# Mixture-of-experts stage: plain float32 products on unsplit weights, in column tiles, experts ranked on chip by their row count

## The reference, cut to what matters

```python
g_sel = jnp.argmax(g_logits, axis=-1)
e_in = jnp.take_along_axis(e_logits, g_sel[:, None, None], axis=1)[:, 0]
top_v, top_i = lax.top_k(e_in, TOP_K)                       # TOP_K = 2
expert_id = g_sel[:, None] * EXPERTS_PER_GROUP + top_i      # 32 experts
combine = jnp.sum(one_hot(expert_id, N_EXPERTS) * w_top[..., None], axis=1)
hg = jnp.einsum('td,edf->tef', t, w_gate)                   # d = 1024, f = 256
hu = jnp.einsum('td,edf->tef', t, w_up)
act = jax.nn.silu(hg) * hu * combine[:, :, None]
y = jnp.einsum('tef,efd->td', act, w_down)
```

## Time and profile before

| | us |
|---|---|
| median of 3 runs (1365.02 to 1366.16) | 1366.15 |
| span of the profiled execution, first to last instruction | 1363.2 |
| TensorE busy, share of the span | 1309.7, 96% |
| expert stage, first product to last | 1028.3 to 1344.6 |
| behind the last product | 18.6 |

### The profile page before, as it was taken

The page is one execution under the profiler, slowest core; times in us unless marked ns, Lnnn a source line. Parts: engine busy times, 40 slices in busy tenths (PEclk is TensorE's granted clock), DMA queues, the critical chain, the costliest instruction groups (busy, mean ns, idle before and its releaser), DMA issues.

```text
span 1363.2 us, 23818 instructions
## 1 busy us (share of the span) xinstructions
PE 1309.7 (96%) x9405; PEld 1202.4 (88%) x9405; DVE 1032.2 (76%) x1535; ACT 872.8 (64%) x1289; POOL 78.2 (6%) x81
## 2 busy tenths in 40 slices
PE   7999999999999999999999899999998999999994
PEld 7989999998999998999999888999986777777773
DVE  6776655568555568998998886874569999999994
ACT  6565444546444546675656766654457999999994
POOL 0001000001000000000001100110000111011113
PEclk9999999999999999999999999999999999999997
DMA  8644555553655544555435534454436999999963
GB/s 276 205 152 130 191 185 185 185 186 94 202 185 187 187 140 145 178 161 158 150 102 181 193 122 155 155 186 161 157 156 254 365 360 354 351 366 365 362 261 123
DMA packets 150108, 279.78 MB, mean 205 GB/s; under 512 B 13721, under 2 KB 122238, under 8 KB 136574
## 3 DMA queue, kind: packets, MB, share of 16 engines
q1 hardware_dynamic: 141952, 269.97, 57.0%
q0 software_dynamic: 7696, 8.41, 2.0%
q10 hardware_dynamic: 366, 0.12, 0.0%
HBM read 274.26 MB, written 21.50 MB: 217 GB/s over the span
## 4 chain that ended last, share of the span: by engine, by line
PE 75%; DVE 15%; ACT 5%; issue 3%; DMA 1%; ACTq 0%; DVEq 0%; POOLq 0%; POOL 0%; SPq 0%
PE psum L852 18%; PE psum L854 18%; PE psum L853 18%; DVE weights_parts L2692 3%; PE psum L1413 3%; PE psum L1412 3%; PE psum L1411 3%; DVE weights_parts L2086 2%; PE psum L1437 2%; DVE arena L2476 2%; PE psum L1439 2%; PE psum L1438 2%; ACT weights_parts L1933 1%; ACT weights_parts L1476 1%; PE psum L1256 1%
## 5 line engine op out<-in xcount | busy, mean ns | idle before, releaser
L2086 DVE TENSOR_TENSOR weights_parts<-ring,weights_parts 128x1024 fp32r<-128x1024 f32 (+3 forms) x312 | 363.4, 1184 | 161.5 <-ACT weights_parts L1476 161.1
L1476 ACT ACTIVATE weights_parts<-ring 128x1024 fp32r<-128x1024 f32 (+3 forms) x312 | 309.0, 1010 | 175.6 <-PE psum L854 174.8
L852 PE MATMUL psum<-xnorm_parts,weights_parts 128*128 128x256 f32 x884 | 255.5, 289 | 6.0 <-DVE xnorm_parts L2235 2.0
L853 PE MATMUL psum<-xnorm_parts,weights_parts 128*128 128x256 f32 x884 | 249.0, 282 | 0.0
L854 PE MATMUL psum<-xnorm_parts,weights_parts 128*128 128x256 f32 x884 | 248.9, 282 | 0.0
L852 PE MATMUL psum<-expert_cols,weights_parts 128*128 128x256 f32 (+1 forms) x688 | 194.7, 283 | 3.3 <-DVE expert_cols L2104 2.0
L854 PE MATMUL psum<-expert_cols,weights_parts 128*128 128x256 f32 (+1 forms) x688 | 192.1, 279 | 0.0
L853 PE MATMUL psum<-expert_cols,weights_parts 128*128 128x256 f32 (+1 forms) x688 | 191.9, 279 | 0.0
L852 PE MATMUL psum<-hidden_parts,weights_parts 128*128 128x256 f32 x640 | 181.9, 284 | 2.6 <-DVE hidden_parts L2544 1.7
L853 PE MATMUL psum<-hidden_parts,weights_parts 128*128 128x256 f32 x640 | 180.5, 282 | 0.0
L854 PE MATMUL psum<-hidden_parts,weights_parts 128*128 128x256 f32 x640 | 180.5, 282 | 0.0
(11 more groups left out here) (422 smaller groups left out, 2528.3 us busy)
## 6 DMA issues: line engine op xcount, KB each, us to landing
expert_raw<-in_w_exp_down SPq DMA_DIRECT2D x35, 1024.0 KB, 7.6
ring<-in_mlp_w_up SPq DMA_DIRECT2D x32, 1024.0 KB, 5.4
ring<-in_mlp_w_down SPq DMA_DIRECT2D x32, 1024.0 KB, 4.9
ring<-in_w_in SPq DMA_DIRECT2D x30, 1024.0 KB, 5.3
ring<-in_w_exp_gate SPq DMA_DIRECT2D x23, 1024.0 KB, 5.0
ring<-in_w_exp_up SPq DMA_DIRECT2D x23, 1024.0 KB, 7.3
ring<-in_attn_w_qkv SPq DMA_DIRECT2D x12, 1024.0 KB, 8.4
expert_raw<-in_w_exp_gate SPq DMA_DIRECT2D x12, 1024.0 KB, 5.0
```

The source lines that it names most:

```text
L852: pe.matmul(out, lh, rh, start=start, stop=False, **more)
L853: pe.matmul(out, lh, rl, start=False, stop=False, **more)
L1476: ins = act.activation(high, src, ACT.Copy)
L2086: ins = dve.tensor_tensor(low, src, high.bitcast(F32), ALU.subtract)
```

## The change

The stage no longer splits the weights. Each product is a plain float32 matmul on the loaded matrix, with the expert's rows as the stationary operand and the weights as the moving one.

A block now has 64 or 32 rows. The output of a 64-row block takes half of the array's columns, so two products stand side by side: for `gate_up` gate in columns 0 to 63 and up in 64 to 127, each with 256 moving columns; for `down` the two halves of the result with 512 each. A 32-row block has four such column tiles, with 128 moving columns in `gate_up` and 256 in `down`.

Expert 0 is fixed at first place, rank 0, and loaded ahead of the routing. The other 31 are ranked on chip by row count. The expert of rank r has at most 512 / r rows, so a fixed table gives each rank its blocks: four of 64 rows for ranks 0 to 2, three for rank 3, two for ranks 4 and 5, one of 64 and one of 32 for ranks 6 and 7, one of 64 for ranks 8 to 15, one of 32 for ranks 16 to 31. That is 47 blocks, 29 of 64 rows and 18 of 32, all of them always run. `ORDER` mixes large and small ranks. Each expert is loaded once, from an address that SP reads from `expert_ids`; five buffers hold a whole expert each, partly in the space that the parts took.

```diff
+ORDER = [0, 17, 18, 3, 19, 8, 1, 20, 21, 9, 22, 10, 2, 23, 24, 11, 4, 25, 12, 5, 26, 13, 6, 27, 14, 7, 28, 15, 16,
+         29, 30, 31]
...
+def blocks_of(rank):
+
+    blocks, off, most = [], 0, most_rows(rank)
+    while off < most:
+        size = 32 if rank >= STATIC and most - off <= 32 else 64
+        blocks.append((off, size))
+        off += size
+    return blocks
...
+            def load_expert(i, e):
+
+                buf, use = i % RAW_BUFS, i - RAW_BUFS
+                if use >= 0:
+                    sp.wait_ge(s["gate_up_done"], tiles_upto(LAST_BLOCK[use] + 1))
+                for dst, w in zip(raw[buf], (wg, wu)):
+                    sp.dma_start(dst, w[e].rearrange("o p n -> p (o n)")).then_inc(pair_in[buf], 16)
+                if use >= 0:
+                    sp.wait_ge(s["down_done"], tiles_upto(LAST_BLOCK[use] + 1))
...
             sp.wait_ge(s["lo_ready"], 2 * len(SPLIT))
-            load_pair(1)
-            load_pair(2)
...
+            sp.wait_ge(s["experts_ready"], 1)
+            for i in range(STATIC, NE):
+                n = FIRST_BLOCK[i]
+                load_expert(i, bass.ds(sp.value_load(expert_ids[0:1, n:n + 1], min_val=0, max_val=NE - 1), 1))
...
-                        x_high, x_low = xe[:, n % 2, 0, kk, :], xe[:, n % 2, 1, kk, :]
-                        pe.matmul(bank2(n % 2), x_high, high[:, :, k, :], start=(kk == 0), stop=False)
-                        pe.matmul(bank2(n % 2), x_low, high[:, :, k, :], start=False, stop=False)
-                        mm = pe.matmul(bank2(n % 2), x_high, low[:, :, k, :], start=False, stop=(kk == KT - 1))
...
+                for k in ks:
+                    if n == 0:
+                        pe.wait_ge(s[f"sorted_out{k % 2}"], k // 2 + 1)
+                    for i in range(b.parts):
+                        p0 = i * b.size
+                        src = raw[buf][i // half][:, k * DE + i % half * width:k * DE + (i % half + 1) * width]
+                        mm = pe.matmul(bank(4 + n % 2)[p0:p0 + b.size, 0:width], x_cols[:, k, :], src,
+                                       start=(k == 0), stop=(k == KT - 1), skip_group_check=True)
...
+                for k in range(2):
+                    for i in range(b.parts):
+                        p0 = i * b.size
+                        mm = pe.matmul(bank(n % Y_KEPT)[p0:p0 + b.size, 0:width], acts[:, n % 2, k * b.size:(k + 1) * b.size],
+                                       raw[buf][2][:, k * D + i * width:k * D + (i + 1) * width],
+                                       start=(k == 0), stop=(k == 1), skip_group_check=True)
...
-            def unit_low(i):
-
-                _, src, high, low = unit_views(*UNIT_ORDER[i])
-                dve.wait_ge(s["unit_high"], i + 1)
-                dve.tensor_tensor(low, src, high.bitcast(F32), ALU.subtract).then_inc(s["unit_low"], 1)
...
+            def window(n):
+
+                b = BLOCKS[n]
+                if n - WINDOWS_KEPT >= N_STATIC:
+                    dve.wait_ge(s["gate_up_done"], tiles_upto(n - WINDOWS_KEPT + 1))
+                at = dve.value_load(window_ids[0:1, n:n + 1], min_val=0, max_val=ROUTED - b.size)
+                dve.tensor_copy(window_of(b), by_place[:, :, bass.ds(at, b.size)]).then_inc(s["window_made"], 1)
```

More of the change, by code:

```diff
@@ L1376, in _, with sorted_part @@
-            warm(16)
+            pe.matmul(bank(b)[:, 2 * NE:3 * NE], ones_bits, mask_bits[:, 1, :], start=False, stop=False,
+                      skip_group_check=True)
+            for tb in range(TB):
+                mm = pe.matmul(bank(b)[0:NE, 3 * NE:3 * NE + 1], mask_bits[:, tb, :], ones_bits[:, 0:1], start=False,
+                               stop=(tb == TB - 1), skip_group_check=True)
+            mm.then_inc(full[b], 1)
+            def sorted_part(k, tb, half):
+                part = nat_parts[:, half, tb, :].rearrange("p (q k) -> p k q", k=KT)[:, k, :]
+                first, last = tb == 0 and half == 0, tb == TB - 1 and half == 1
+                return pe.matmul(bank((4 + k) % 8), part, sort[:, tb, :], start=first, stop=last, skip_group_check=True)
@@ L1377, in _ @@
+            warm(4)
+            pe.wait_ge(s["chosen_ready"], 1)
+            pe.wait_ge(s["nat_copied"], TB)
+            pe.matmul(bank(3)[0:1, 0:NB], ones[0:NE, 0:1], chosen_of, start=True, stop=True).then_inc(s["chosen_full"], 1)
+            warm(10)
+            pe.wait_ge(s["nat_high"], 1)
+            pe.wait_ge(s["sort_ready"], TB)
+            pe.wait_ge(s["experts_ready"], 1)
+            for k in range(KT):
+                sorted_part(k, 0, 0)
             pe.wait_ge(s["nat_low"], 1)
-            pe.wait_ge(s["sort_ready"], TB)
@@ L1389, in _ @@
[L1389 to L1401 removed]
+            for k in range(KT):
+                sorted_part(k, 1, 0)
+                if k == 0:
+                    pe.wait_ge(s["nat_low"], TB)
+                sorted_part(k, 1, 1).then_inc(s["sorted_full"], 1)
@@ new lines, in spans, with gate_up @@
+            def spans():
+                pe.wait_ge(s["sorted_out1"], 2)
+                pe.wait_ge(s["spans_ready"], 1)
+                for i, src in enumerate((starts_of, ends_of, ranks_of)):
+                    mm = pe.matmul(bank(7)[:, i * NB:i * NB + src.shape[1]], ones[0:NE, :], src, start=(i == 0),
+                                   stop=(i == 2), skip_group_check=True)
+                mm.then_inc(s["spans_full"], 1)
+            def gate_up(b, ks):
+                n, buf = b.n, b.expert % RAW_BUFS
+                if ks[0] == 0:
+                    pe.wait_ge(pair_in[buf], 32 * (b.expert // RAW_BUFS + 1))
+                    if b.rank >= STATIC:
+                        pe.wait_ge(s["window_made"], n - N_STATIC + 1)
@@ L2916, in _ @@
+            dve.wait_ge(s["windows_ready"], 1)
+            for n in range(NB):
+                gated(BLOCKS[n])
+                if n == 0:
+                    mixing_weights()
+                if n == 1:
+                    late_rows()
+                while made_windows[0] < min(max(n + 1, N_STATIC) + WINDOWS_KEPT, NB):
+                    window(made_windows[0])
+                    made_windows[0] += 1
             dve.wait_ge(s["final_in"], 16)
```

550 lines of the change are left out of this document (233 added, 317 removed).

## The result

The changed kernel takes 1295.3 us, the one before 1366.15: a ratio of 0.9478, with a 95% interval of 0.9465 to 0.9492. It is 5.2% faster, 9.7 us better than the 1305 forecast and inside the range. Four of its five executions lie between 1293.2 and 1296.6 (their median is 1294.4), and the fifth, the profiled one, ran in a slower state at a lower clock (0.82) and took 1404.4. A difference of about 1 us from 1295.3 says nothing. The profile of after shown here is that of another run of the same kernel, e1_again: 1299.93 us, 4.6 above the median. Of these, 2.6 us were lost ahead of the stage, as a comparison under e10_all shows.

What follows compares the result with a forecast made beforehand. The DMA engines were taken to bound the stage, TensorE close behind (1269): last landing 1276.3, plus 4 hold-ups and 4 last block, last product 1284; plus 18.6 tail and 2.95 to the timed run, 1305 us, range 1290 to 1318.

Steps and rivals of the forecast that it cites:

- Rate: Ranked expert loads: 97.5 MB at 388 GB/s take 251.3 us, plus 7 for indirect transfers.
- Start of the loads: After the ranking: first load at 1015.7, data from 1018.0; each us of delay is one at the end.
- Hold-ups: Expert stage, TensorE and loads waiting on each other through buffers: 4 us added.
- 64-row block: TensorE, two column tiles fully overlapping: 5.7 us per block, 166 us for 29.
- 32-row block: TensorE, four column tiles: 4.4 us per block, between 3.1 and 5.7; 79 us for 18.
- Last block: End of the expert stage: 4 us for the block that can only be finished after its loads.
- Tail: From the last product to the end of the span: 18.6 us, unchanged.
- Span to timed run: Step from profile span to timed result: the median of the runs stands 2.95 us above the span.
- TensorE as the bound for want of overlap: Expert stage: four tiles go no faster than two, or little better than none; 1315 to 1360, taken 1330; chance 0.22.
- Slow loads: Expert loads: the DMA engines keep 8.94 us per expert; 1325 us; chance 0.10.
- Tiles one after the other: TensorE: column tiles with wide moving operands do not overlap, 10.8 us per block; 1554 us; chance of slower 0.08.
- The quicker case: Expert stage: fewer hold-ups and loads at 400 GB/s; 1290 us; chance 0.08.

Runs made afterwards that it cites:

- e1_again: The changed kernel as it is, block-size rule only written in other words, run again for its profile: 1299.93 us.
- e10_all: Changed kernel with e9's rank order and products of zeros, plus e8's down products first in the last four blocks: 1299.5 us, ratio 0.9513.
- e4: Changed kernel without four of the eight k steps of gate and up, all loads kept: 1289.6 us, ratio 0.9438.
- e7: Changed kernel fetching only half of the down matrix for the later experts with a 32-row block: 1281.1 us, ratio 0.9379.
- e2: Changed kernel with all 47 blocks at 64 rows, so no four-tile blocks: 1310.8 us, ratio 0.9593.
- e3: Changed kernel with gate and up of 64-row blocks one after the other in the same column tile: 1374.0 us, ratio 1.0063.
- e11: Changed kernel fetching all down matrices in 8 KB pieces, also those of experts with a 32-row block: 1295.4 us, ratio 0.9487.
- e6: Changed kernel loading fixed experts without waiting for the ranking: 1294.9 us, ratio 0.9480.
- e5: Changed kernel with ranks 3 and 7 exchanged in `ORDER`: 1289.7 us, ratio 0.9449.
- e8: Changed kernel with the former block's down products ahead of gate and up in the last four blocks: 1294.5 us, ratio 0.9476.
- e9: e5's order on the changed kernel, plus ten products of zeros ahead of each of the last five blocks: 1291.9 us, ratio 0.9459.
- e12: e10_all with the four early gathers moved behind the last store: 1303.0 us, ratio 0.9535.

## Why the prediction was right, step by step

*The mechanism holds.* Splitting is gone, TensorE and the DMA engines are left, the loads set the end (e4, e7), TensorE is close behind (e2), tiles overlap (e3, rows of e1_again). The last load was forecast to land at 1276.3 + 4 of hold-ups = 1280.3; in e1_again the last "up" landed at 1268.9, and all but 0.2 MB of the loads had moved by then. That the sum came within 10 us is partly luck, for its terms were off in both directions:

- *Rate, mis-sized.* 388 GB/s came from stretches averaged with their gaps; the engines do 415 at a share of 1.02. And bytes were missing: with 2.05 MB of indirect transfers, 0.5 MB of norm weights and 0.4 MB of instructions the 97.5 MB are 100.5, 242.1 us at 415, against 251.3 + 7 in the sum: 16.2 too many. Per full share that is 407, not 388, and why the same engines gave less before stays open; piece size isn't it (e11).
- *Start of the loads.* 1017.6 against 1015.7: masks 1.6 us later in this profile, 3.9 us from masks to load against 3.6. From profile to profile it moves, 1015.0 in e5, e8 and e11, 1017.2 in e2 and e4. But its weight was wrong: e6 shows that 14 us of earlier start are worth 0 where the text had 1:1. The cover was named in the next paragraph (expert 5 behind four blocks) and not drawn into the sum: a load that must wait for a buffer anyway gains nothing when the queue begins earlier.
- *Hold-ups.* Taken 4, measured 6.8, one hole at 1096 to 1103; e5 removes it and gets 5.6. With start and rate: 1280.3 + 1.9 - 16.2 + 2.8 = 1268.8, as measured.
- *64-row block.* 5.7 forecast, 5.59 measured. *32-row block.* 4.4 taken, 3.0 measured: the low end, 3.1, was right. The earlier trace rows had shown full overlap at two tiles, and the step to the middle was caution without a row. TensorE alone would end near 1026 + 29 x 5.59 + 18 x 3.0 = 1242, or near 1248 by e2 (last product at 1290.2, less the 42 us), not 1269. The Trainium skill ("TensorE: Matmul & The Clock Gate", section Part 3) has 2.38 times for three tiles; four gave four-fold here, so the measurement decides.
- *Last block, mis-sized.* Taken 4 us from the last landing to the last product, measured 9.4 in e1_again, 8.5 in e11, 7.6 in e6, 7.1 in e8 and 6.5 in e5. The clock named as a risk "only inside a large expert" matters most here: at 1.2 GHz the last small one takes nearly twice as long, and nothing covers it.
- *Tail.* 18.6 forecast; 18.6 in e8, 19.0 in e5, 19.7 in e6, 19.8 in e11 and e1_again. *Span to timed run.* 1.7 to 1.9 us in nearly all runs that show both (2.3 in two), not 2.95: the profile of before was itself a run about 1.1 under its median.
- *Rounding.* The text's own terms, 1276.3 + 4 + 4 + 18.6 + 2.95, make 1305.85, not 1305.

Together, for e1_again: 1305.85 + 1.9 - 16.2 + 2.8 + 5.4 (last block) + 1.2 (tail) - 1.1 = 1299.85, against 1299.93. The median run, 1295.3, is 4.6 quicker. The nearest profile, e11 with 1295.8, has its loads 2.6 us earlier, 0.6 less between there and the last landing, and 0.9 less in the last block.

*The rivals.* TensorE as the bound for want of overlap: refuted by 27 ns a record, though e2 shows how near it is. Slow loads: refuted by 415 GB/s. Tiles one after the other: e3 made it true for gate and up of the 64-row blocks alone and landed at 1374. The quicker case (1290), given 0.08, had the load rate nearer (400) and the hold-ups and last block too small.

## What to carry to other kernels

Where two engines pace each other through buffers, cost the first half by the one that frees buffers and the second by the one that fills them: a us saved at the start of the loads is worth nothing if a buffer is awaited later, while a hole in them in the middle is lost for good, and the order of large and small pieces decides whether there is one. Read a transfer rate from a stretch in which the engines are full, not from an average divided by a share. And look at what the waiting engine's clock does to the one block that nothing covers.

## What the runs showed of the hardware

- Four 32-column tiles of plain float32 products run four-fold: groups of four records with 128 columns follow each other at 0.107 us at 2.4 GHz, and 64 records with the weight loads take 1.95 us; moving operands may come from different buffers.
- Four indirect gathers (some 1.8 MB) beside short products at full clock cost the chain 4 to 4.5 us (e9, e10, e1_again), in gaps between TensorE's records and in a late start of ScalarE's silu, which no semaphore explains; without them (e12) both are gone. Beside wider products at full clock (e2) there are none.
- 2.1 us of products of zeros ahead of each of the last blocks hold the granted clock at 1.00 from 1250 to 1275, where it had fallen to 0.74 in e5. Here they ran on behind the landing of the data and gained nothing.
